# Expert outputs added one expert later, and expert tokens fetched from memory by row number

## The reference

```
h   = rms_norm(x) * (1 + sc2) + sh2
idx = top 2 experts of the best group, gates = their scores, normalised
y   = sum over the token's experts e of gate_e * ((silu(h @ w1[e]) * (h @ w3[e])) @ w2[e])
x   = x + g2 * y
```

## Time and profile before

| | us |
|---|---|
| median of 3 runs | 1671.23 |
| lowest, highest | 1666.68, 1672.34 |
| the profiled execution | 1669.39 |
| its span, first to last instruction | 1667.6 |
| PE busy | 1538.4 (92%) |
| DVE busy | 712.8 (43%) |
| ACT busy | 330.9 (20%) |
| mean granted clock of PE | 0.974 |

### The profile page before, as it was taken

How to read it: one execution, slowest core, us unless ns; L and a number is a source line. 1 busy time by engine, 2 the same in 40 slices (tenths; PEclk the granted TensorE clock), 3 DMA queues, 4 the chain that set the end, 5 groups by cost and what they waited for, 6 DMA issues and landing times.

```text
span 1667.6 us, 21507 instructions
## 1 busy us (share of the span) xinstructions
PE 1538.4 (92%) x7910; PEld 688.8 (41%) x7911; DVE 712.8 (43%) x2050; ACT 330.9 (20%) x539; POOL 0.2 (0%) x4
## 2 busy tenths in 40 slices
PE   6999999978898999999989799896999998999996
PEld 3454555643343333333333355453333333333332
DVE  3325665342424433434343548725334342434343
ACT  4322222030101101011111357413011110111111
POOL 0000000000000000000000000000000000000000
PEclk9999999989999999999999899997999999999999
DMA  9437776840868999999968501424799995999992
GB/s 347 156 107 297 263 262 235 341 163 1 326 280 334 426 427 426 426 426 425 427 278 328 202 0 51 202 101 164 299 403 426 427 425 235 426 426 424 428 425 123
DMA packets 67564, 495.66 MB, mean 297 GB/s; under 512 B 4464, under 2 KB 21120, under 8 KB 28224
## 3 DMA queue, kind: packets, MB, share of 16 engines
q1 hardware_dynamic: 66048, 489.33, 71.9%
q10 hardware_dynamic: 1472, 5.72, 1.0%
HBM read 493.45 MB, written 1.58 MB: 297 GB/s over the span
## 4 chain that ended last, share of the span: by engine, by line
PE 87%; DVE 6%; ACT 4%; issue 2%; ACTq 0%; DVEq 0%
PE PS L755 84%; PE PS L759 2%; DVE misc L1763 1%; ACT hT L545 1%; DVE xc L1705 1%; DVE halves L1525 0%; DVE misc L1525 0%; DVE halves L1516 0%; DVE halves L1518 0%; ACT hT L738 0%; DVE halves L1517 0%; DVE hT L1753 0%; ACT hT L530 0%; ACT hT L516 0%; ACT halves L662 0%
## 5 line engine op out<-in xcount | busy, mean ns | idle before, releaser
L755 PE MATMUL PS<-halves,hT 128*64 128x512 f32 x3072 | 676.5, 596 | 20.4 <-ACT hT L545 17.4
L755 PEld LDWEIGHTS PS<-halves,hT 128*64 128x64 f32 x3072 | 223.9, 137 | 441.1 <-issue 436.7
L755 PE MATMUL PS<-hT,halves 128*128 128x384 f32 x640 | 219.2, 498 | 8.4 <-ACT halves L628 6.5
L1705 DVE SCALAR_TENSOR_TENSOR xc<-PS,MOD,xc 128x128 f32<-128x128 f32 x592 | 195.8, 408 | 40.2 <-PE PS L755 40.2
L755 PEld LDWEIGHTS PS<-hT,halves 128*128 128x128 f32 x640 | 121.8, 194 | 106.9 <-issue 23.3
L1753 DVE TENSOR_TENSOR hT<-hT,PS 128x512 f32<-128x512 f32 x32 | 22.0, 687 | 276.1 <-ACT hT L530 276.1
L755 PE MATMUL PS<-h,hT 128*64 128x512 f32 x408 | 106.1, 660 | 20.8 <-DVE xc L1705 13.0
L755 PE MATMUL PS<-halves 128*128 128x384 f32 (+1 forms) x336 | 118.5, 512 | 0.7 <-ACT pre L575 0.7
L1763 DVE COPY misc<-PS 128x512 f32<-128x512 f32 x32 | 22.1, 691 | 216.5 <-PE PS L755 216.5
L530 ACT ACTIVATE hT<-PS 128x512 f32<-128x512 f32 x32 | 19.1, 597 | 452.2 <-PE PS L755 452.2
L755 PE MATMUL PS<-hT,misc 64*128 64x384 f32 x512 | 91.2, 495 | 9.3 <-DVE misc L1763 9.3
(11 more groups left out here) (232 smaller groups left out, 1091.0 us busy)
## 6 DMA issues: line engine op xcount, KB each, us to landing
halves<-in_moe_w SPq DMA_DIRECT2D x192, 2048.0 KB, 14.9
halves<-in_ada_w SPq DMA_DIRECT2D x48, 1024.0 KB, 6.6
halves<-in_hy_w_in SPq DMA_DIRECT2D x12, 1024.0 KB, 5.2
halves<-in_rg_w_in SPq DMA_DIRECT2D x4, 2048.0 KB, 15.5
halves<-in_hy_w_out SPq DMA_DIRECT2D x4, 1024.0 KB, 8.1
halves<-in_rg_w_out SPq DMA_DIRECT2D x2, 2048.0 KB, 9.6
halves<-in_rg_wa SPq DMA_DIRECT2D x1, 2048.0 KB, 10.9
halves<-in_rg_wx SPq DMA_DIRECT2D x1, 2048.0 KB, 13.4
```

The source lines that it names most:

```text
L755: return nc.tensor.matmul(out, lhsT, rhs, start=start, stop=stop)
L1705: ins = v.scalar_tensor_tensor(xc[:, k, cs], PS[:, bank, cs], MOD[:, l, 8 * G2 + k, s:s + 1], xc[:, k, cs], ALU.mult, ALU.add)
```

## The change

Four edits, all in the experts' part.

1. **Tokens by row number.** At the start of a layer GpSimd writes `h` to a tensor in memory, as 768 rows of half a token (2 KB). `pick` is widened to 128 columns (the 64 slots twice). Half way through the gate products of expert e PE multiplies `pick` of expert e+1 with the tokens' row numbers, three products of one column, into bank 6. DVE adds 1 for the upper half and converts to integers, and GpSimd fetches 128 rows into `xg` with one indirect DMA. Only the first expert of a layer is still gathered by PE.
2. **The token transposes** move into the second products, ahead of step 6 of 8.
3. **The combine of expert e** moves to after the gate products of expert e+1: six products, then the transposes of hid and gpick, then two products. Its banks change (`SPREAD_BANKS`), and so do those of the transposes (2 and 3). DVE adds the results after it has made hid. The last expert's combine stands after the loop.
4. **The release** of the w1 and w3 slots is raised by the first transpose of hid in place of the first matmul of the gather.

The core of the diff:

```diff
+            for l in range(LAYERS):
+                for t in range(NT):
+                    pool_.wait_ge(S("tok"), before("tok", l) + 2 * t + 2)
+                    pool_.dma_start(tokens[l][2 * P * t:2 * P * t + 2 * P, :].rearrange("(p j) c -> p (j c)", j=2),
+                                    h[:, t, :]).then_inc(S("tok_out"), 16)
+                pool_.wait_ge(S("tok_out"), 16 * NT * (l + 1))
+                for e in range(NE):
+                    pool_.wait_ge(S("rows"), before("rows", l) + e + 1)
+                    pool_.wait_ge(S("xT_mm"), before("xT_mm", l) + e + 1)
+                    pool_.indirect_dma_start(xg, None, tokens[l], bass.IndirectOffsetOnAxis(rows_i, 0)) \
+                        .then_inc(S("xg_in"), 16)
...
+                def combine(k, bank):
+                    g, c = k // 4, k % 4
+                    mm(PS[:, bank, 0:N], yo[m * g:m * g + m, P * c:P * c + P], gpT[m * g:m * g + m, :], True, True) \
+                        .then_inc(S("c_mm"), 1)
+
+                def spread(l, e, passes_done, lo, hi):
+
+                    for i in range(lo, hi):
+                        if i == 0:
+                            pe.wait_ge(S("acc_done"), added(l, e))
+                        if i == 3:
+                            pe.wait_ge(S("x_acc"), 8 * passes_done + 1)
+                        if i >= 6:
+                            pe.wait_ge(S("acc_done"), added(l, e, i - 4))
+                        combine(COMBINE[i][0], SPREAD_BANKS[i])
...
                         pe.wait_ge(S("xT"), before("xT", l) + e + 1)
-                        pe.wait_ge(S("acc_done"), before("acc_done", l) + 8 * e + 2)
...
+                            if k == 3:
+
+                                pe.wait_ge(S("yo"), GATED + before("yo", l) + e)
+                                pe.wait_ge(S("pick"), before("pick", l) + e + 2)
+                                for t in range(NT):
+                                    rows_mm = mm(PS[:, 6, 0:1], pick[:, t, :], const("token_rows")[:, t:t + 1],
+                                                 t == 0, t == NT - 1)
+                                rows_mm.then_inc(S("G_mm"), 1)
                         last.then_inc(S("w13_mm"), 1)
+
+                        pe.wait_ge(S("rows"), before("rows", l) + e + 1)
                         with pe.If(extra > 0):
                             with pe.Fori(0, extra) as j:
                                 extra_pass(r, group, e, done + j)
-                        pe.wait_ge(S("pick"), before("pick", l) + e + 2)
-                        pe.wait_ge(S("acc_done"), before("acc_done", l) + 8 * e + 6)
-                        gather(l, 0, 2, pick, HALF, S("w13_last")).then_inc(S("G_mm"), 1)
+                        if r:
+                            spread(l, e, done + extra, 0, 6)
+                        else:
+                            with pe.If(group > 0):
+                                spread(l, e, done + extra, 0, 6)
+                        pe.wait_ge(S("x_acc"), 8 * (done + extra) + 1)
                         pe.wait_ge(S("hid"), before("hid", l) + e + 1)
                         for c in range(4):
-                            last = tr(PS[:, 5, P * c:P * c + P], chunk(hid, c))
+                            last = tr(PS[:, 2, P * c:P * c + P], chunk(hid, c))
+                            if c == 0:
+                                last.then_inc(S("w13_last"), 1)
...
-                        pe.wait_ge(S("acc_done"), before("acc_done", l) + 8 * e + 8)
+                        pe.wait_ge(S("acc_done"), added(l, e, 1))
                         for k in range(KD):
                             half = k // 4
                             if k % 4 == 0:
                                 arrived(4 + half, r, group)
+                            if k == 6:
+                                pe.wait_ge(S("xg_in"), 16 * NE * l + 16 + e * 16)
+                                pe.wait_ge(S("acc_done"), added(l, e, 5))
+                                for c in range(4):
+                                    last = tr(PS[:, 1, P * c:P * c + P], xg[:, P * c:P * c + P])
+                                last.then_inc(S("xT_mm"), 1)
...
-                        pe.wait_ge(S("xg"), before("xg", l) + e + 2)
-                        for c in range(4):
-                            last = tr(PS[:, 1, P * c:P * c + P], xg[:, P * c:P * c + P])
-                        last.then_inc(S("xT_mm"), 1)
-
-                        pe.wait_ge(S("yo"), before("yo", l) + e + 1)
                         pe.wait_ge(S("gpT"), before("gpT", l) + e + 1)
...
+                    dve.wait_ge(S("G_mm"), before("G_mm", l) + e + 2)
+                    ch.link(v.tensor_scalar(rows_f, PS[:, 6, 0:1], const("upper"), None, ALU.add))
+                    v.tensor_copy(rows_i, rows_f).then_inc(S("rows"), 1)
...
-                    dve.wait_ge(S("G_mm"), before("G_mm", l) + e + 2)
-                    v.tensor_copy(xg, PS[:, 0, :]).then_inc(S("xg"), 1)
+                    with dve.If(e > 0):
+                        add_output(l, e, SPREAD_BANKS, done + extra)
```

More of the change, by code:

```diff
@@ L80, in constants @@
     put("desc", np.tile(NE - np.arange(NE), (P, 1)))
+    put("token_rows", 2 * (np.arange(P)[:, None] + P * np.arange(NT)[None, :]))
+    put("upper", (np.arange(P) >= BASE)[:, None])
     put("limits", np.tile(BASE + EXTRA * np.arange(NX), (P, 1)))
@@ L126 @@
 PER = dict(sq=8, ss_mm=1, rms=1, rinv=1, rb_mm=1, nrm=8, hT_act=BY_ACT, hT_dve=KD - BY_ACT, ada_mm=12, o_mm=8, x_upd=8,
-           rt_mm=3, rt_ev=1, rt_exp=1, rt_max=1, rt_mask=1, tok_mm=6, tok=6, route=1, pick=17, gpick=17, G_mm=17, xg=17,
+           rt_mm=3, rt_ev=1, rt_exp=1, rt_max=1, rt_mask=1, tok_mm=6, tok=6, route=1, pick=17, gpick=17, G_mm=17, xg=1, rows=16,
            xT_mm=17, xT=17, w13_mm=16, sig=16, hid=16, gpT_mm=16, gpT=16, hidT_mm=16, hidT=16, w2_mm=16, yo=16,
-           c_mm=128, acc_done=136)
+           c_mm=128, acc_done=128)
 def before(name, index):
@@ L142, in moe_slot, with added @@
     return c + 6 * r if c < 2 else c
+def added(l, e, tiles=0):
+    return ADDED - 8 + before("acc_done", l) + 8 * e + tiles
 def freed(l, slot):
@@ L316, in cut @@
             return region[:, at:at + n]
-        pick = cut(hT, 0, NT * BASE).rearrange("p (t r) -> p t r", t=NT)
+        pick = stack[:, 0, :].rearrange("p (t r) -> p t r", t=NT)
+        rows_f = stack[:, 1, 0:1]
+        rows_i = stack[:, 1, 1:2].bitcast(mybir.dt.uint32)
+        tokens = [nc.dram_tensor(f"tokens{l}", (2 * N, HALF), F32, kind="Internal").ap() for l in range(LAYERS)]
         gpick = cut(hT, 192, NT * P).rearrange("p (t r) -> p t r", t=NT)
@@ L709, in _ @@
                 else:
-                    norm(2, "acc_done", before("acc_done", l) - 7)
+                    norm(2, "acc_done", ADDED + before("acc_done", l) - 7)
                     mixer1()
@@ L1072, in gather @@
                     for g in range(groups):
-                        last = mm(PS[m * g:m * g + m, bank, 0:width], picked[:, t, :],
+                        last = mm(PS[m * g:m * g + m, bank, 0:width], picked[:, t, 0:m],
                                   h[:, t, width * g:width * g + width], t == 0, t == NT - 1)
-                        if begun is not None and t == g == 0:
-                            last.then_inc(begun, 1)
                 return last
@@ L1186, in expert_layer @@
                         last.then_inc(S("w2_mm"), 1)
-                        pe.wait_ge(S("xg"), before("xg", l) + e + 2)
-                        for c in range(4):
-                            last = tr(PS[:, 1, P * c:P * c + P], xg[:, P * c:P * c + P])
-                        last.then_inc(S("xT_mm"), 1)
-                        pe.wait_ge(S("yo"), before("yo", l) + e + 1)
-                        pe.wait_ge(S("gpT"), before("gpT", l) + e + 1)
-                        pe.wait_ge(S("x_acc"), 8 * (done + extra) + 1)
-                        for k, bank in COMBINE:
-                            g, c = k // 4, k % 4
-                            if bank == 1:
-                                pe.wait_ge(S("xT"), before("xT", l) + e + 2)
-                            mm(PS[:, bank, 0:N], yo[m * g:m * g + m, P * c:P * c + P], gpT[m * g:m * g + m, :], True, True) \
-                                .then_inc(S("c_mm"), 1)
+                        pe.wait_ge(S("gpT"), before("gpT", l) + e + 1)
+                pe.wait_ge(S("yo"), GATED + before("yo", l + 1))
+                pe.wait_ge(S("acc_done"), added(l, NE))
+                for k, bank in COMBINE:
+                    if bank == 1:
+                        pe.wait_ge(S("xT"), before("xT", l + 1))
+                    combine(k, bank)
             for l in range(LAYERS):
@@ L1210, in _ @@
                 expert_layer(l)
-            pe.wait_ge(S("acc_done"), before("acc_done", LAYERS))
+            pe.wait_ge(S("acc_done"), added(LAYERS, 0) + 8)
             pe.wait_ge(S("xT"), before("xT", LAYERS))
@@ L1707, in add_expert, with add_output @@
```

(9 more changed lines are left out.)

43 lines of the change are left out of this document (26 added, 17 removed).

## The result

The kernel after takes 1690.8 us (median of 4 runs, 1689.1 to 1694.8), the kernel before in the same session 1670.3 (1666.7 to 1672.3). The ratio is 1.0108, 95% interval 1.0088 to 1.0128: slower by about 1.1%, 18 us by the ratio and 20 by the medians. Forecast were 1677 and slower by 6. The sign, the stream as the bound and the period of 30.2 us came as forecast; the size is three times too small. The profiled execution took 1690.85 us with a span of 1689.0, 21.4 more than the span before.

The account below looks back on a forecast made before the run. PE sets the pace now, only a few us ahead of a full weight stream, which would bind after. Layer 0's -1 and layer 1's +7 give +6 us on 1669.39, 1675.4; plus 1.84 for the median, 1677; range 1663 to 1697.

Parts of the forecast that it names:

- What bounds: Ordinary experts: PE's period falls from 28.82 to 26.95 us, but the weight stream, with the fetch, needs 30.2 us.
- The fetch's bytes: Each expert's token fetch adds 0.262 MB, 0.66 us, to the full weight stream; 24.5 fetches lie on the chains.
- B: Rival: fetch packets fill bubbles between weight loads and cost the stream little; at no cost 1661 us; chance 0.2.
- C: Rival: the fetch costs more than its bytes because one DMA engine falls behind; 1685 to 1700 us; chance 0.2.
- Stretch 1: Layer 0 to expert 2's extra pass: PE's gain counts, -6.5 us at the pass's end, next pair issued at -3.8.
- the shorter way to expert 1: Layer 0, after expert 0: the next expert starts sooner, -3.0 to -5 us.
- +0.8 at expert 13: Layer 0, experts 3 to 13: the weights land at 818.2 against 817.4 now, so all of PE's gain is gone.
- The release: Gate slots freed later: nothing in mid-stream, but after an extra pass the pair is issued 2.7 to 3.1 us later.
- +1.8 after the pass: Layer 0, behind expert 13's extra pass: PE's second products start 8.7 us after the pass instead of 6.94.
- Layer 0's end: After expert 13's pass: -3.0 at the next start, -1.9 for expert 14, +0.9 at expert 15; layer ends at -1.
- stretch 3: Layer 1 to expert 7's pass: first pair issued 3.0 us later, fetches added, +0.1 us against PE's time now.
- stretch 4: Expert 7's pass to the end: +4.3 for weights, 1.5 for the clock, 0.6 and 0.7 for expert 15; together +7.

Follow-up runs that it names:

- e9_peel: The kernel after, with TensorE's first two experts of each layer written ahead of the loop, without pass code at expert 1 and layer 1's expert 0: 1684.2 us.
- e11_release_peel: The kernel after with the edits of e2_release and e9_peel together: 1674.9 us, ratio 1.0015 to the kernel before.
- e2_release: The kernel after, with the w1 and w3 slots released by a transpose of its own right after the gate products or extra passes: 1680.4 us.
- e10_before_peel: The kernel before, with e9_peel's edit (first two experts of each layer written out on TensorE): 1679.9 us, ratio 1.0040.

## Why the forecast was right in sign and too small

**What bounds.** Right. PE's new period without waits is 27.41 us (26.95 forecast, chiefly because the row products take 0.83 instead of 0.5, the gap before the second products 4.95 instead of 4.7). It is seen in the experts behind the start of a layer and behind a pass. The others run at 211.4 / 7 = 30.2 us, the forecast's number.

**The fetch's bytes** (24.5 x 0.66 = 16 us). Right. The total rate didn't rise with the second queue, so B is out; seven eighths of the bytes removed gave 10 us with the other delays in place and 12 without them, against 14, with 14 inside both intervals. For C nothing speaks: the period isn't above 30.2, and PE never waited for the tokens. The Trainium skill's page "DMA: Bandwidth & Descriptors", section "Latency and other measured facts", says that engines 7 and 15 are usually slower, and gives GpSimd's descriptor rings as a best guess at the cause, not as certain; my forecast told the guess as if it were a rule. No period here shows such a delay.

**Stretch 1** (-6.5 us at the end of expert 2's pass, the pair behind it at -3.8) is the step that failed: the pass ended at -0.3, its pair was issued at +3.9, and the second products behind it began at +2.0. The pass's last products and the issue of the pair, before and after:

```profile
501.25 1.57 PE L755 MATMUL PS<-misc 32*128 32x384 f32 x16 [0.55 <-DVE misc L1721]
506.97 8.56 SPq L359 DMA_DIRECT2D halves<-in_moe_w  x3
```

```profile
500.98 1.57 PE L788 MATMUL PS<-misc 32*128 32x384 f32 x16 [0.55 <-DVE misc L1798]
510.85 0.81 SPq L376 DMA_DIRECT2D halves<-in_moe_w  x2
```

Of the 7.7 us between -3.8 and +3.9, 6.2 arose before the pass's end and 1.4 in the release. Expert 1 was to gain 1.9 us and lost 2.9. My sum carried the old kernel's 2.31 us of late instructions over as if the new code had the same; it had 4.16, and behind them the lower clock on transposes (1.77 us) and second products (8.8 us instead of 7.8). Besides, the shorter way to expert 1 gave 2.3 us where the forecast had -3.0 to -5, and its -6.5 needs the -5. The full stream then handed the loss on, so "+0.8 at expert 13" became +8.0. e9_peel shows it: with those instructions on time the pass ends at -7.7 and expert 13 is at +2.9. With the early release besides (e11_release_peel) expert 13 is at +0.4, beside the forecast's +0.8.

**The release** (2.7 to 3.1 us later, at two passes). Right mechanism, undersized term. It was 8.3 us behind the pass, not 6.9, since the waits for the adds also lowered the clock (PEclk 0.50 from 855 to 860 us, the row below, in the columns of the earlier one; in the kernel before it was 1.00 all through this part). That is 3.6 to 4.5 us later than before, not 2.7 to 3.1. In e2_release it was 3.0 us behind the pass, and that edit, at all places together, took 10.7 us off. The forecast's "+1.8 after the pass" was +3.9.

```profile
855.00:860.00 5.00, 4.28 (x13) 2.40 (x13) 4.96 (x19) 0.07 (x1) 0.00 (x0) 0.50 0.00 0
```

**Layer 0's end, stretch 3 and stretch 4.** Forecast -1, +0.1 and +7. Relative to where each began, layer 0's end was +1.5 against -1.8, the start of layer 1 brought 1.4 more, stretch 3 was +2.4 against +0.1, and stretch 4 +8.1 against +6.9. Together with the 7.2 us at expert 13 these make the 15 us by which the forecast fell short.

Stretch 3 can be followed in the traces. TensorE had 2.22 us of late instructions at expert 1 of layer 1, but 2.11 before, so it lost nothing by them itself. What changed is what stands behind them: before, the slots were freed by the gather, issue at 1209.6; now they are freed only behind six combines:

```profile
1219.28 3.32 PE L788 MATMUL PS<-hT,misc 64*128 64x384 f32 x12 [2.22 <-issue]
1223.19 0.83 SPq L376 DMA_DIRECT2D halves<-in_moe_w  x2
```

By then the stream had run dry: the third load of the next expert landed 7.3 us behind the second, not 4.9. These 2.4 us are the whole of what stretch 3 missed by; the loads before them landed as forecast, and the periods behind them are 30.2 us. No run removes this moment alone.

**Rival E** (PE doesn't gain) is out for ordinary experts, and partly true for the first ones.

## What to carry to other kernels

Where two engines are within a few per cent of each other, work taken off the one pays only until the other binds: price the change by the stream's bytes, its dry stretches and the order in which it waits for slots. Before taking work off an engine, ask what that work covered: the gather beside a wait kept TensorE's clock up and was worth more than its 2.75 us. A load that an earlier release frees is followed by the next one in the queue's order, so look at what frees that one too. And don't carry a stall named "issue" over to changed code: rewritten code has its own.

## What I had not expected of the hardware

- Code that TensorE runs for the first time can arrive 2 to 4 us late (4.16, 2.31, 3.23 us), each time 2.3 to 2.9 us behind the start of a 16 KB instruction packet, and in a layout changed elsewhere the lateness turns up at another expert. The same edit was worth +6 us on one kernel (e10_before_peel) and -6 us on the other (e9_peel).
- At some places 1.2 to 2.2 us without work brought the granted clock to 0.61 to 0.65 over the next 4.4 to 4.7 us and added 1.6 us to 32 products; 1.01 us did not, and neither did waits of 1.8 to 2.0 us at other experts nor the 2.59 us behind expert 13's pass in the kernel before. But 2.59 us behind expert 2's pass there did: the gather took 4.49 us, not 2.75. So the forecast was wrong to read the earlier trace rows as the one such place. The length of one gap alone doesn't tell. Thirteen transposes of the identity (1.64 us) were enough to prevent it.
- An indirect fetch of 128 rows of 2 KB beside a full stream landed 6.8 to 7 us after its issue, held GpSimd for 0.95 us, and displaced just its own bytes.
